# 32 bytes of padding ahead of a shared SBUF region in a two-block transformer kernel

## The chip, the cores and the metric

One core of a Trainium2 chip. The metric is the device time of one execution in microseconds; the kernel before takes 2682.19 us (median of 3 runs, 2679.93 to 2685.24).

## The reference, cut to what matters

The reference is a three-layer stack on 512 latent tokens (x) and 256 context tokens (ctx), model width 1024, everything in fp32. The first block does adaptive layer norm, windowed attention with a context, a gated delta rule in both directions, a gated merge and a squared-ReLU MLP. The second block is two layers of differential attention, a pooling mixer and the same MLP:

```
def sq_relu_mlp(h, w1, w2):
    return jnp.square(jax.nn.relu(h @ w1)) @ w2          # 1024 -> 4096 -> 1024

x = x.astype(jnp.float32) + gt1 * merge(y_attn, o_dl, dz, ga, gd)     # first block
x = x + gt2 * mlp(x, sh2, sc2)
...
for l in range(2):                                                    # second block
    u, q, k, v = split_heads(h @ w_in[l])
    ...
    x = x + ga * (mix @ w_out[l])
    x = x + gm * sq_relu_mlp(modulate(rms_norm_2(x, g_mlp[l]), sm, cm), w_mlp1[l], w_mlp2[l])
    if not last:                                                      # the same for ctx
```

So most of the arithmetic is dense products of 1024-wide activations with weights, 512 columns wide for x and 256 wide for ctx.

## The kernel before

**How a dense product is made.** Activations lie feature-major: a tensor [128, 2, 8, n] holds 8 tiles of 128 features by n tokens, twice, as a high part and a low part in fp32r (index 0 and 1 of the second axis). Weights come in blocks of 128x4096 into one of three slots of `raw` (`sync_loads`, line 301, on SP's queue). ScalarE copies a piece of 128x1024 to the high part in `ws` (line 318), VectorE subtracts to get the low part (line 326), and TensorE multiplies (`product`, line 328 on, matmul at line 337): for each of 8 k-tiles three matmuls, high by high, high by low, low by high, each with a weight load of its own.

```
for a, b in ((lh, rh), (lh, rl), (ll, rh)):
    m = e.matmul(o, a, b, start=n == 0, stop=n == 3 * kt - 1)
```

The first operand `a` is the stationary one (128x128), the second `b` is the moving one (512 or 256 columns). The profile writes a matmul as `ps<-moving,stationary`. A piece is thus 24 matmuls of 512 columns for x, and 24 of 256 for ctx where both streams run. `pe_tiles` (lines 367 to 369) and the parts of products that run beside attention (lines 949 to 951 and 2463 to 2465) make the same three matmuls from other lines. At line 2190 the roles are turned: the weights `ws` move (512 columns) and slices of the activations `hh` or `hc` are stationary.

**Where things lie.** `build` allocates fixed tensors one after another, and behind them one region of 73728 bytes a partition, which every stage lays out anew (`region`, line 138): `ar` and `ar2` (loose fp32 scratch: q, k, v, softmax rows, delta rule), `hc1`/`hc2` (the normed ctx, shown as `hc`), `gg`/`g2` (the hidden layer of the MLPs and the merge's input, shown as `gg` and `g`), `gc2` (hidden layer of ctx, shown as `gc`), `yy` (the merged output) and `ctx2`. The program's own addresses, bytes from the start of a partition:

| tensor | address | modulo 64 |
|---|---|---|
| raw, ws, hh, xT, cst | 16512, 65664, 90240, 123008, 139392 | 0 |
| rs, sq, mi | 149056, 151104, 155200 | 0 |
| the region: ar, ar2, hc1, gg, g2 | 155232 | 32 |
| yy and gc2; hc2; ctx2 | 188000; 204384; 220768 | 32 |

`mi` is 32 bytes long, so what follows it begins 32 bytes past a multiple of 64. Every tensor of the region and every slice of 16 floats' step in it is therefore 32 bytes off; the fixed ones are not, but for `par2`, a small table of parameters.

**The order of the work.** Each engine's program is a Python function that runs through the stages in turn; the order is written out by hand, and semaphore waits are the only link between engines. The two engines that prepare `ws` work up to three pieces ahead (`WSN = 3`). Stages by the trace: inputs and q, k, v of the first block (0 to 140 us), attention (to 310), delta rule (to 635), merge and output (to 815), the first MLP (to 1181), then for each layer of the second block products, attention, output product, MLP: 1181 to 2050 with both streams, and 2050 to 2676 with x alone.

Of the kernel before, what the change touches and what calls it, by code (L numbers as in the profile page):

```python
# [15 lines left out]
P = 128  # L16
# [85 lines left out]
def build(nc, I, out):  # L102
    ctx = ExitStack()
    with ctx:
# [15 lines left out]
        def sb(name, shape, dt=F32, stack=ctx):  # L120
            return stack.enter_context(nc.sbuf_tensor(name, shape, dt))
# [11 lines left out]
        rs = sb("rs", [P, T])  # L133
        sq = sb("sq", [P, 2, T])
        mi = sb("mi", [P, 8])
        REST = 18432

        def region(names):
            st = ExitStack()
            got = [sb(n, s, dt, st) for n, s, dt in names]  # L140
            st.close()
            return got

        ar, = region([("ar", [P, REST], F32)])
        hc1, = region([("hc1", [P, 2, KT, TC], F32R)])
        gg, yy = region([("gg", [P, 2, KT, T], F32R), ("yy", [P, 2, KT, T], F32R)])
        ar2, hc2, ctx2 = region([("ar2", [P, REST - 6144], F32), ("hc2", [P, 2, KT, TC], F32R),
                                 ("ctx2", [P, KT, TC], F32)])
# [421 lines left out]

        YA = REST - 2048
        cx = ar[:, YA:YA + 2048].rearrange("p (k n) -> p k n", k=KT)
# [2429 lines left out]
```

## Time and profile before

| | |
|---|---|
| median of 3 runs | 2682.19 us (2679.93 to 2685.24) |
| span of the profiled execution, first to last instruction | 2676.4 us |
| median less span | 5.8 us |
| mean granted TensorE clock | 0.978 |
| busy: PE, VectorE, ScalarE, GpSimd | 94%, 58%, 35%, 4% |
| chain that ended last: PE, VectorE, ScalarE, DMA | 85%, 9%, 2%, 1% |

The span is the profiler's, from the first to the last instruction; the runs' times take in what lies around it. A matmul's duration in the trace is not its share of the engine: matmuls are pipelined, each one's record lasts until its last column is out, and the next has begun long before. What a matmul costs in a saturated stretch is the distance from one start to the next, and in the view in order of time it is found as (start of the next row less start of this one) divided by the count of this row.

### The profile page before, as it was taken

The page shows a single profiled execution, that of the slowest core. Times are in us where ns is not written, and L with a number is a line of the kernel's source. Part 1 is how long each engine was busy: PE and PEld are TensorE (multiplying, and loading weights), DVE is VectorE, ACT ScalarE, POOL GpSimd, SP SyncE. Part 2 cuts the span into 40 slices and gives each one's busy share as a digit, 9 for nine tenths or more (in the row PEclk, how much of TensorE's full clock was granted, in tenths as well). Part 3 has the DMA queues.
Part 4 walks back from the last instruction along what each step waited for, and adds up shares of the span by engine and source line. Part 5 has one row for each costly group of instructions (what it writes and reads, how often), then busy time and mean ns, then how long its engine had stood idle before and what let it go on. Part 6 is the DMA issues. An engine that isn't in the chain of part 4 may idle for free.

```text
span 2676.4 us, 45804 instructions
## 1 busy us (share of the span) xinstructions
PE 2521.2 (94%) x19622; PEld 2039.4 (76%) x19622; DVE 1557.1 (58%) x2412; ACT 931.9 (35%) x1599; POOL 115.6 (4%) x222
## 2 busy tenths in 40 slices
PE   6999988779999999999998999999999998999997
PEld 3777667667887788877777888888887776788886
DVE  3355577767656788854675556545445466534444
ACT  3344443223235223342553432222233254422322
POOL 0000001120100010000000000000000000000000
PEclk8999899989999999999999999999999999999999
DMA  6000000004653555411002123333321102222210
GB/s 277 32 32 1 33 3 4 5 5 172 221 214 118 181 189 190 172 44 59 5 32 79 64 95 126 126 126 126 126 95 44 63 32 86 93 97 103 95 63 32
DMA packets 32202, 244.88 MB, mean 91 GB/s; under 512 B 3616, under 2 KB 3776, under 8 KB 20992
## 3 DMA queue, kind: packets, MB, share of 16 engines
q1 hardware_dynamic: 11808, 164.83, 15.4%
q0 software_dynamic: 20192, 77.11, 9.1%
q8 instruction: 157, 2.57, 0.4%
q14 instruction: 45, 0.37, 0.0%
HBM read 239.83 MB, written 2.10 MB: 90 GB/s over the span
## 4 chain that ended last, share of the span: by engine, by line
PE 85%; DVE 9%; issue 3%; ACT 2%; DMA 1%; POOL 0%; DVEq 0%; SPq 0%; ACTq 0%
PE ps L337 57%; PE ps L2190 2%; PE ps L2419 2%; PE ps L949 1%; PE ps L2447 1%; PE ps L1370 1%; PE ps L2463 1%; PE ps L905 1%; PE ps L367 1%; PE ps L2465 1%; PE ps L2464 1%; PE ps L368 1%; PE ps L369 1%; PE ps L950 1%; PE ps L951 1%
## 5 line engine op out<-in xcount | busy, mean ns | idle before, releaser
L337 PE MATMUL ps<-hh,ws 128*128 128x512 f32 x3216 | 752.9, 393 | 10.9 <-DVE hh L524 7.1
L337 PEld LDWEIGHTS ps<-hh,ws 128*128 128x128 f32 x3216 | 601.3, 188 | 144.9 <-issue 15.6
L318 ACT ACTIVATE ws<-raw 128x1024 fp32r<-128x1024 f32 x295 | 308.6, 1049 | 430.0 <-PE ps L337 396.6
L326 DVE TENSOR_TENSOR ws<-raw,ws 128x1024 fp32r<-128x1024 f32 x295 | 359.8, 1221 | 151.5 <-ACT ws L318 151.4
L337 PE MATMUL ps<-g,ws 128*128 128x512 f32 x1536 | 364.4, 396 | 0.0
L337 PEld LDWEIGHTS ps<-g,ws 128*128 128x128 f32 x1536 | 286.4, 188 | 66.6
L337 PE MATMUL ps<-gg,ws 128*128 128x512 f32 x960 | 227.6, 398 | 2.1 <-ACT ws L318 2.1
L1807 DVE SCALAR_TENSOR_TENSOR xT<-ps,mods,xT 128x512 f32<-128x512 f32 x120 | 90.0, 750 | 227.8 <-PE ps L337 220.5
L337 PEld LDWEIGHTS ps<-gg,ws 128*128 128x128 f32 x960 | 181.3, 189 | 46.4 <-ACT ws L318 2.5
L1970 DVE TENSOR_TENSOR sq<-sq 128x512 f32<-128x512 f32 (+1 forms) x128 | 80.0, 625 | 142.4 <-ACT sq L1947 142.4
L1947 ACT ACTIVATE sq<-ps 128x512 f32<-128x512 f32 (+1 forms) x128 | 69.4, 542 | 258.7 <-PE ps L337 244.6
L337 PEld LDWEIGHTS ps<-hc,ws 128*128 128x128 f32 (+1 forms) x1032 | 129.2, 188 | 6.8 <-ACT hc L506 1.5
L337 PE MATMUL ps<-hc,ws 128*128 128x256 f32 (+1 forms) x1032 | 132.2, 284 | 1.4 <-ACT hc L506 1.1
L1880 DVE CUSTOM_DVE_ANT_0 ar<-ar,par 128x1024 f32<-128x1024 f32 x96 | 122.8, 1279 | 3.5
L337 PEld LDWEIGHTS ps<-gc,ws 128*128 128x128 f32 x768 | 95.4, 188 | 2.8
L337 PE MATMUL ps<-gc,ws 128*128 128x256 f32 x768 | 96.0, 281 | 0.0
L468 ACT ACTIVATE sq<-xT 128x512 f32<-128x512 f32 x48 | 30.3, 632 | 184.1 <-DVE xT L1807 184.1
L2638 DVE TENSOR_REDUCE mvec<-ps 128x1 f32<-128x768 f32 (+1 forms) x80 | 64.3, 846 | 51.7 <-PE ps L2419 51.3
L2564 ACT ACTIVATE raw<-ps,mvec 128x768 f32<-128x768 f32 (+1 forms) x80 | 64.5, 811 | 70.5 <-DVE mvec L2638 70.5
L1880 DVE CUSTOM_DVE_ANT_0 raw<-raw,par 128x1024 f32<-128x1024 f32 x64 | 81.9, 1279 | 2.8 <-DVE mods L1880 0.5
L1621 ACT ACTIVATE raw<-ps 128x512 f32<-128x512 f32 x60 | 35.5, 592 | 106.4 <-PE ps L1387 81.4
L1974 DVE TENSOR_TENSOR g<-sq,g 128x512 fp32r<-128x512 f32 x64 | 44.3, 693 | 44.8 <-ACT g L1950 44.8
(378 smaller groups left out, 3571.1 us busy)
## 6 DMA issues: line engine op xcount, KB each, us to landing
raw<-in_w_m SPq DMA_DIRECT2D x32, 2048.0 KB, 7.8
raw<-in_w_ada POOLq DMA_DIRECT2D x80, 512.0 KB, 3.9
raw<-in_w_mlp SPq DMA_DIRECT2D x16, 2048.0 KB, 8.0
ar<-in_w_ada POOLq DMA_DIRECT2D x48, 512.0 KB, 3.9
raw<-in_w_in SPq DMA_DIRECT2D x8, 2048.0 KB, 7.4
raw<-in_w_mg SPq DMA_DIRECT2D x8, 1536.0 KB, 7.3
raw<-in_w_out SPq DMA_DIRECT2D x6, 2048.0 KB, 8.1
raw<-in_w SPq DMA_DIRECT2D x5, 2048.0 KB, 7.5
```

What stands on the lines that cost most here:

```text
L318: e.activation(w_of(n)[0], pieces[n][2], ACT.Copy).then_inc(*hi(n))
L326: e.tensor_tensor(l, pieces[n][2], h.bitcast(F32), ALU.subtract).then_inc(*lo(n))
L337: m = e.matmul(o, a, b, start=n == 0, stop=n == 3 * kt - 1)
L1807: e.scalar_tensor_tensor(x[:, mt, 0:w], ps[name][:, 0:w], gain, x[:, mt, 0:w], ALU.mult, ALU.add).then_inc(*dve(name))
L1880: e.tensor_tensor_reduce(junk, w[t % n], cb[:, j * 1024:j * 1024 + 1024], 1.0, Q2("bada", l)[:, t:t + 1], ALU.mult, ALU.add, mods[:, 1 + l ...
L1947: e.activation(r, ps[tag, "u", q, m, j][:, 0:w], ACT.Relu).then_inc(*act((tag, "u", q, m, j)))
L1970: e.tensor_tensor(r, r, r, ALU.mult).then_inc(*dve((tag, "r2", i)))
L1974: e.tensor_tensor(hid[:, 1, m, :], r, hid[:, 0, m, :].bitcast(F32), ALU.subtract).then_inc(*dve(((tag, "hid", q, j), m)))
L2190: mm = e.matmul(ps[l, "v", i], a, b[:, kk, :], start=k == 0 and a is xh and b is h, stop=k == 7 and a is xl)
L2419: m = e.matmul(ps.two((l, "s2", i, p))[:, a:b], q, kall[halves(p), t4, a:b], start=True, stop=True)
L2564: e.activation((e_buf[i % 2], e_second)[p][:, 0:n], ps.two((l, "s2", i, p))[:, 0:n], ACT.Exp, bias=(nm0, nm1)[p], accum_out=(su0, su1)[p]) ...
L2638: e.reduce_max(nm[p], ps.two((l, "s2", i, p))[:, 0:cols_of(i)], AXX, negate=True).then_inc(*dve((l, "m2", i, p)))
```

## The change

One tensor is allocated that nothing writes or reads. It is 8 floats, 32 bytes a partition, between `mi` and the region.

```
--- before.py
+++ after.py
@@ -133,6 +133,7 @@
         rs = sb("rs", [P, T])
         sq = sb("sq", [P, 2, T])
         mi = sb("mi", [P, 8])
+        sb("line", [P, 8])
         REST = 18432
 
         def region(names):
```

By the program's own addresses `line` gets 155232, the region now begins at 155264, and all that lies in it is 32 bytes further on: yy and gc2 at 188032, hc2 at 204416, ctx2 at 220800, all multiples of 64. Everything ahead of it stays where it was. No instruction is added, removed or moved, on any engine or queue; line numbers from 136 on are one higher.

## Rows read from the trace of the kernel before

**Rows 1.** The page: busy time by engine, and the chain that ended last by engine.
```profile
PE 2521.2 (94%) x19622; PEld 2039.4 (76%) x19622; DVE 1557.1 (58%) x2412; ACT 931.9 (35%) x1599; POOL 115.6 (4%) x222
...
PE 85%; DVE 9%; issue 3%; ACT 2%; DMA 1%; POOL 0%; DVEq 0%; SPq 0%; ACTq 0%
```

**Rows 2.** The chain in order of time, its longest pieces (start, us, what).
```profile
914.33 172.99 PE ps L337 x744
...
1519.65 516.87 PE ps L337 x2964
...
2316.43 254.15 PE ps L337 x1104
```

**Rows 3.** Busy time by stretch: us and instructions, granted clock, DMA share, GB/s.
```profile
1800.00:2000.00 200.00, 200.00 (x1150) 175.45 (x1148) 98.10 (x148) 53.31 (x82) 10.55 (x20) 1.00 0.35 119
```

**Rows 4.** PE in order of time, last MLP: start us, us, op, shape, count.
```profile
2348.91 44.96 PE L337 MATMUL ps<-g,ws 128*128 128x512 f32 x192
2393.71 43.71 PE L337 MATMUL ps<-hh,ws 128*128 128x512 f32 x192
2437.25 44.96 PE L337 MATMUL ps<-g,ws 128*128 128x512 f32 x192
```

**Rows 5.** PE in order of time, end of the merge and the output product.
```profile
746.81 11.07 PE L337 MATMUL ps<-hh,ws 128*128 128x512 f32 x48
757.71 5.76 PE L337 MATMUL ps<-gg,ws 128*128 128x512 f32 x24
763.31 44.96 PE L337 MATMUL ps<-yy,ws 128*128 128x512 f32 x192
```

**Rows 6.** PE in order of time, value product of the second block, line 2190.
```profile
1216.61 2.95 PE L2190 MATMUL ps<-ws,hc 128*128 128x512 f32 x12
1219.40 5.61 PE L2190 MATMUL ps<-ws,hh 128*128 128x512 f32 x24
1224.85 2.95 PE L2190 MATMUL ps<-ws,hc 128*128 128x512 f32 x12
```

**Rows 7.** PE in order of time, MLP with both streams.
```profile
1561.07 5.65 PE L337 MATMUL ps<-hh,ws 128*128 128x512 f32 x24
1566.56 3.00 PE L337 MATMUL ps<-hc,ws 128*128 128x256 f32 x24
1569.40 5.76 PE L337 MATMUL ps<-g,ws 128*128 128x512 f32 x24
```

**Rows 8.** Groups by form, TensorE: count, busy us, mean ns, idle before.
```profile
L337 PE MATMUL ps<-g,ws 128*128 128x512 f32 x1536 | 364.4, 396 | 0.0
...
L337 PE MATMUL ps<-gg,ws 128*128 128x512 f32 x960 | 227.6, 398 | 2.1 <-ACT ws L318 2.1
...
L337 PE MATMUL ps<-hc,ws 128*128 128x256 f32 x1008 | 129.2, 284 | 1.4 <-ACT hc L506 1.1 <-DVE hc L524 0.2
...
L337 PE MATMUL ps<-gc,ws 128*128 128x256 f32 x768 | 96.0, 281 | 0.0
...
L2190 PE MATMUL ps<-ws,hc 128*128 128x512 f32 x96 | 24.4, 403 | 0.0
...
L2464 PE MATMUL ps<-hc,ws 128*128 128x256 f32 x72 | 20.2, 281 | 0.0
```

**Rows 9.** Groups by form, plain fp32 products and transposes of the attention.
```profile
L2447 PE MATMUL ps<-raw,ar 128*128 128x128 f32 x416 | 53.5, 276 | 1.3 <-ACT raw L2573 1.3
...
L2432 PE MATMUL ps<-cst,raw 128*128 128x128 f32 x208 | 30.2, 273 | 4.4 <-ACT ar L2582 2.5 <-DVE mvec L2648 1.2 <-DVE raw L2654 0.7
```

**Rows 10.** Groups by form, VectorE: one operation on either kind of tensor.
```profile
L1880 DVE CUSTOM_DVE_ANT_0 ar<-ar,par 128x1024 f32<-128x1024 f32 x96 | 122.8, 1279 | 3.5
...
L1880 DVE CUSTOM_DVE_ANT_0 raw<-raw,par 128x1024 f32<-128x1024 f32 x64 | 81.9, 1279 | 2.8 <-DVE mods L1880 0.5
...
L1970 DVE TENSOR_TENSOR sq<-sq 128x512 f32<-128x512 f32 x96 | 66.4, 692 | 125.9 <-ACT sq L1947 125.9
...
L1974 DVE TENSOR_TENSOR g<-sq,g 128x512 fp32r<-128x512 f32 x64 | 44.3, 693 | 44.8 <-ACT g L1950 44.8
```

**Rows 11.** The page, DMA issues: KB each, us from issue to landing.
```profile
raw<-in_w_ada POOLq DMA_DIRECT2D x80, 512.0 KB, 3.9
...
ar<-in_w_ada POOLq DMA_DIRECT2D x48, 512.0 KB, 3.9
```

More of the change, by code:

```diff
@@ L135, in build @@
         mi = sb("mi", [P, 8])
+        sb("line", [P, 8])
         REST = 18432
```

## Prediction, made before the changed kernel ran

> **What bounds the kernel now.** I read the page first, then the chain, then the work of TensorE in order of time. The page has TensorE busy 94% of the span, and the chain that ended last is 85% TensorE, 9% VectorE, 1% DMA [rows 1]. The chain in order of time says where: its longest pieces are the dense products of line 337, and in them the chain doesn't leave TensorE for 173, 517 and 254 us [rows 2]. In one stretch of 200 us inside the longest, TensorE is busy all 200 at a granted clock of 1.00, VectorE 98, ScalarE 53, the DMA engines 35% [rows 3]. In these stages nothing but the rate of the matmuls counts, and each nanosecond of a matmul comes through to the end.
>
> The change adds no instruction and moves none. It shifts the region by 32 bytes. So the one question is whether an engine or a DMA reads or writes a tensor faster at a multiple of 64 bytes than 32 bytes off it. The trace of before can answer it, since it has both kinds of tensor under the same operations.
>
> **TensorE, 512 columns.** In the last MLP stretches of 192 matmuls with `g` moving (32 off) alternate with 192 with `hh` moving (a multiple of 64). Same line, same shape, same weights buffer, no idle time. `g`: (2393.71 - 2348.91) / 192 = 233.3 ns each; `hh`: (2437.25 - 2393.71) / 192 = 226.8 ns [rows 4]. The difference is 6.5 ns, 2.8%. Is it the address or the phase of the MLP? In the merge the two alternate piece by piece: `hh` (757.71 - 746.81) / 48 = 227.1 ns, `gg` (763.31 - 757.71) / 24 = 233.3 ns; and `yy`, another tensor of the region with other work beside it, has 44.96 us for 192 matmuls, to the hundredth what `g` has [rows 5, 4]. The best control is line 2190, where the activations are the stationary operand and the moving one is `ws` both times: with slices of `hc` (32 off) (1219.40 - 1216.61) / 12 = 232.5 ns, with slices of `hh` (1224.85 - 1219.40) / 24 = 227.1 ns [rows 6]. So it is enough that either operand is 32 off. I take the 6.5 ns of the longest stretches.
>
> How many: 1536 with `g`, 960 with `gg`, 192 with `yy`, 96 with `hc` stationary [rows 8, 5], 2784 in all, with no idle time before them but 2.1 us. Saved: 2784 x 6.5 ns = 18.1 us. The operands after it have the same place against 64 bytes as `hh` and `ws` have now.
>
> A rule that speaks against a part of it: the Trainium skill, "SBUF — State Buffer", section "Who interferes with whom", gives TensorE two read ports, one for the moving operand and one for weight loads, independent of each other. By that the 96 matmuls with only the stationary operand off would have nothing to gain, and this term would be 17.5 us. The rows of line 2190 speak against it.
>
> **TensorE, 256 columns.** 1008 with `hc` and 768 with `gc` at line 337, and nine rows like that of line 2464 (three of 72, three of 64, three of 48, 552 matmuls) [rows 8]: 2328. All of them move a tensor that is 32 off, at (1569.40 - 1566.56) / 24 = 118.3 ns [rows 7]; no row shows one at a multiple of 64, so this price is bounded. Upper end: the same 6.5 ns for each, a fixed cost of a start, 15.1 us. Other end: 512 columns at 2.4 GHz are 213.3 ns, so an aligned matmul of 512 pays 13.5 ns over its columns, one that is off 20.0, and the narrow one pays 118.3 - 106.7 = 11.6. If the 13.5 were a fixed price of an aligned matmul, the narrow one would go to 120.2, 1.9 ns slower, a loss of 4.4 us. Between them I take the price in proportion to the columns, half of 6.5 or 3.3 ns: the narrow matmul's 11.6 is near half of the wide one's 20.0, not near the whole. 2328 x 3.3 = 7.7 us. The 360 of them at lines 949 to 951 and 2463 to 2465 stand among attention steps that wait for softmax, so I leave their 1.2 us out: 6.5 us.
>
> **TensorE, plain fp32.** The products of the second attention with a stationary operand in `ar` take 276 ns in the record, transposes of the same size with both operands in fixed tensors 273 [rows 9]. At most 416 x 3 ns = 1.2 us; half of it is on the path at best, 0.6 us. The small matmuls of the delta rule (64 columns) have no like pair, and their stage waits for VectorE step by step; nothing is put down for them.
>
> **A side effect.** After a run of `hc` the next run of `hh` takes (1566.56 - 1561.07) / 24 = 228.8 ns, not 226.8 [rows 7, 4]. It may go too: with 32 pieces of this kind and 24 matmuls each, 2 ns is 1.5 us. It stays out of the sum and in the range.
>
> **VectorE, ScalarE, DMA.** The modulation's dot product takes 1279 ns on `ar` (32 off) and 1279 on `raw` (a multiple of 64) [rows 10], and a transfer of 512 KB lands 3.9 us after its issue in either [rows 11]. Nothing to gain, nothing to lose.
>
> **What is late next.** Per piece of 24 wide matmuls TensorE's time falls from 5.60 to 5.44 us. In the stretch of rows 3 VectorE has half of its time free, so pieces of weights stay ahead and no new wait comes up.
>
> **The sum.** 18.1 + 6.5 + 0.6 = 25.2 us off the profiled execution's span of 2676.4, which gives 2651.2. The median of the runs lies 5.8 us above that span: 2657.0 us, 0.9% faster.
>
> **The rivals.**
>
> *The narrow matmuls gain nothing, or lose.* The terms are then 18.1 + 0.6, less 4.4 at the worst: between 2663.5 and 2667.9 us. For it speaks that their 11.6 ns over the columns are already under the 13.5 of an aligned wide one. Against it, that 20.0 for 512 columns and 11.6 for 256 look like a cost that grows with the columns.
>
> *Nothing changes.* The 6.5 ns would come from where the region lies (all of it is above 155000 bytes) or from something that I haven't thought of that its tensors share. Then the time is 2682.2 us. All tensors of the region are both 32 off and high up, so no row of TensorE separates the two fully; but `g`, `yy` and `hc` lie up to 49 KB apart and cost the same to within 1 ns, which doesn't look like a matter of distance. That the allocation does nothing is ruled out by the program's own addresses.
>
> Beside it a rule: the Trainium skill, "SBUF — State Buffer", section "Specifications (TRN2)", gives SBUF cachelines of 16 bytes. 32 bytes are two whole lines, so by that rule no operand crosses more lines before than after and this rival is right. The rows of TensorE speak against 16 bytes being the only unit that counts.
>
> *Slower: the clock gives it back.* The saturated stretches get 2.8% denser in columns, and if TensorE's granted clock fell there, all matmuls in them would pay. The place is the three stretches of rows 2, 944 us; 0.01 of clock costs 9.4 us, so it decides from a fall of 0.027 on, and a fall of 0.04 would give 2657.0 + 37.6 = 2695 us. Against it: the `hh` stretches already run at this density, and the stretch of rows 3, with TensorE busy all the time, has a granted clock of 1.00.
>
> **How the numbers follow.** Forecast as summed, 0.72. Narrow ones without gain, 0.15. No change, 0.10. Clock, 0.03. The range: the full 6.5 ns for the narrow ones adds 8.6 us, all of the fp32 term 0.6, the side effect 1.5, which is 2646; a little more for the runs' own spread of 3 us gives 2644. Upward the second case reaches 2668, and with that spread 2670. No change and slower are outside, 0.13. Of a measurement of this kernel about 0.2%, 5.4 us, can be told from no change: faster by more than that has the first two cases, 0.87; within it, no change, 0.10; slower, 0.03.
>
> **What would show it.** In the profile after, the `g` stretches of the last MLP should take 43.5 us from start to start for 192 matmuls, as `hh`, not 44.8; line 2190 should show no difference between `hc` and `hh`; a narrow run of 24 should take 2.76 us from start to start (2.84 would be the second case, 2.68 the upper end). VectorE's 1279 ns and the 3.9 us should stand. I am wrong in the mechanism if `g` still takes 233 ns, and wrong in the path if the matmuls get faster and idle time before them takes up what they save, which rows on line 337 with a new wait for `ws` would show.

## The result, and the profile after

The changed kernel takes 2666.3 us (median of 4 runs, 2665.1 to 2670.61), the kernel before 2681.78 us beside it (4 runs, 2679.93 to 2685.24). The ratio is 0.9954, with a 95% interval of 0.9941 to 0.9968: 12.3 us less, between 8.6 and 15.8. The interval leaves out 1, so it is faster, and the time is inside the range, but the gain is about half of the 25 us that were forecast. The profiled execution took 2665.17 us with a span of 2663.4, 13.0 us under the span of before.

The page after: TensorE's busy time is 16.4 us less, and the chain that ended last is on TensorE for 84% of the span, where it was 85%.

```profile
PE 2504.8 (94%) x19622; PEld 2040.8 (77%) x19622; DVE 1556.6 (58%) x2412; ACT 931.4 (35%) x1599; POOL 115.6 (4%) x222
...
PE 84%; DVE 9%; issue 3%; ACT 2%; DMA 1%; POOL 0%; DVEq 0%; ACTq 0%; POOLq 0%
```

The chain in order of time, the three pieces that answer to [rows 2]. They are 2.6, 2.5 and 3.9 us shorter; the middle one, 517 us with narrow matmuls in it, gained least for its length.

```profile
910.43 170.37 PE ps L338 x744
...
1512.01 514.34 PE ps L338 x2964
...
2308.58 250.25 PE ps L338 x1104
```

Busy time in the stretch of [rows 3]. TensorE is as full as it was at a granted clock of 1.00, with VectorE and ScalarE where they were: in this stretch the clock gave nothing back.

```profile
1800.00:2000.00 200.00, 200.00 (x1153) 177.04 (x1152) 97.22 (x145) 52.33 (x80) 10.03 (x19) 1.00 0.33 116
```

TensorE in order of time in the last MLP (start us, us, engine, line, operation, shape, count), which answers to [rows 4]:

```profile
2341.06 43.68 PE L338 MATMUL ps<-g,ws 128*128 128x512 f32 x192
2384.58 43.68 PE L338 MATMUL ps<-hh,ws 128*128 128x512 f32 x192
2428.10 43.68 PE L338 MATMUL ps<-g,ws 128*128 128x512 f32 x192
```

`g` now has (2384.58 - 2341.06) / 192 = 226.7 ns from start to start, as `hh` has, where it had 233.3.

The value product, now line 2191, for [rows 6]: with `hc` stationary (1211.68 - 1208.96) / 12 = 226.7 ns, where it had 232.5.

```profile
1208.96 2.88 PE L2191 MATMUL ps<-ws,hc 128*128 128x512 f32 x12
1211.68 5.60 PE L2191 MATMUL ps<-ws,hh 128*128 128x512 f32 x24
```

The MLP with both streams, for [rows 7]:

```profile
1553.52 5.63 PE L338 MATMUL ps<-hh,ws 128*128 128x512 f32 x24
1558.99 3.04 PE L338 MATMUL ps<-hc,ws 128*128 128x256 f32 x24
1561.86 5.63 PE L338 MATMUL ps<-g,ws 128*128 128x512 f32 x24
```

Here is the surprise: a narrow run of 24 takes 1561.86 - 1558.99 = 2.87 us, 119.6 ns a matmul, where it had 118.3. It got slower.

The groups by form, TensorE (count, busy us, mean ns, idle before), for [rows 8]:

```profile
L338 PE MATMUL ps<-hh,ws 128*128 128x512 f32 x3192 | 745.8, 392 | 11.0 <-DVE hh L525 7.3 <-DVE xT L1808 3.1 <-issue 0.5
...
L338 PE MATMUL ps<-g,ws 128*128 128x512 f32 x1536 | 355.3, 390 | 0.0
...
L338 PE MATMUL ps<-gg,ws 128*128 128x512 f32 x960 | 221.5, 391 | 2.1 <-ACT ws L319 2.1
...
L338 PE MATMUL ps<-hc,ws 128*128 128x256 f32 x1008 | 129.6, 284 | 1.9 <-ACT hc L507 1.1 <-DVE hc L525 0.7
...
L338 PE MATMUL ps<-gc,ws 128*128 128x256 f32 x768 | 97.0, 283 | 0.0
```

From before to after: `g` 364.4 to 355.3, `gg` 227.6 to 221.5, `yy` 45.0 to 43.7, line 2190 with `hc` 24.4 to 23.9 us busy, together 17.0 us less; `hh` 746.8 to 745.8; `hc` 129.2 to 129.6 and `gc` 96.0 to 97.0, 1.4 us more. That is 16.6 us less. The other 552 narrow ones, which stand among steps that wait, show no loss: their groups are busy 166.0 us before and 165.4 after. In the MLP with both streams `g` behind a narrow run takes 227.9 ns after, not 226.7; that is why the wide ones gained 17.0 us and not 18.1.

The span fell by 13.0 us, 3.6 less than the 16.6. In another profiled execution of the same changed kernel (below) the span was 2659.4 us, 4.0 less, and all of these 4.0 lie ahead of 911 us; from there on the two agree to 0.1 us. So a part of the 3.6 can't be told from chance, but one place repeats: from the end of the longest piece of the chain to the value product of the next layer it was 34.2 us before (2036.5 to 2070.7) and is 35.7 in both executions after. A dip of the granted clock lies in it each time, at another place: in the two stretches of 6 us that begin 7.5 us behind the piece it is 0.53 and 0.90 before, 0.75 and 0.78 after. That this is what the 1.6 us are is not shown.

### The profile page after: what moved, and what is told of

It is laid out like the page before. It is cut to its first block, busy times and chain, and to the rows that moved or that the text cites. A ratio compares the mean times of both kernels' runs of the same rounds, so it can differ in the third digit from the quotient of the medians.

```text
span 2663.4 us, 45804 instructions
## 1 busy us (share of the span) xinstructions
PE 2504.8 (94%) x19622; PEld 2040.8 (77%) x19622; DVE 1556.6 (58%) x2412; ACT 931.4 (35%) x1599; POOL 115.6 (4%) x222
## 3 DMA queue, kind: packets, MB, share of 16 engines
q1 hardware_dynamic: 11808, 164.83, 15.5%
## 4 chain that ended last, share of the span: by engine, by line
PE 84%; DVE 9%; issue 3%; ACT 2%; DMA 1%; POOL 0%; DVEq 0%; ACTq 0%; POOLq 0%
PE ps L338 56%; PE ps L2191 2%; PE ps L2420 2%; PE ps L950 1%; PE ps L2448 1%; PE ps L1371 1%; PE ps L2464 1%; PE ps L368 1%; PE ps L906 1%; PE ps L370 1%; PE ps L369 1%; PE ps L2466 1%; PE ps L2465 1%; PE ps L952 1%; PE ps L951 1%
## 5 line engine op out<-in xcount | busy, mean ns | idle before, releaser
L338 PE MATMUL ps<-g,ws 128*128 128x512 f32 x1536 | 355.3, 390 | 0.0
L338 PE MATMUL ps<-gg,ws 128*128 128x512 f32 x960 | 221.5, 391 | 2.1 <-ACT ws L319 2.1
L1881 DVE CUSTOM_DVE_ANT_0 ar<-ar,par 128x1024 f32<-128x1024 f32 x96 | 122.8, 1280 | 3.5
L1881 DVE CUSTOM_DVE_ANT_0 raw<-raw,par 128x1024 f32<-128x1024 f32 x64 | 81.9, 1279 | 2.8 <-DVE mods L1881 0.5
L1371 PE MATMUL ps<-ar,raw 64*64 64x64 f32 x1920 | 44.4, 230 | 29.1 <-DVE ar L1569 22.1
```

What stands on the lines that cost most here:

```text
L1371: m = e.matmul(ps.two(name)[halves(j), 512 * p + 64 * b:512 * p + 64 * b + 64], A[halves(p), 2 * b + j, :], Xt[halves(p), 2 * b + j, :], s ...
L1881: e.tensor_tensor_reduce(junk, w[t % n], cb[:, j * 1024:j * 1024 + 1024], 1.0, Q2("bada", l)[:, t:t + 1], ALU.mult, ALU.add, mods[:, 1 + l ...
```

## The experiments

All kernels keep every instruction in its place and move only addresses, unless said otherwise. "Distance" is the moving operand's address less the stationary one's, modulo 256 bytes; `ws` lies at 128 past a multiple of 256, so it is 224 for the region of before (155232, 96 past a multiple of 256), and 0 for the changed kernel's (155264, 128 past one). In the value product, where the region's tensor is the stationary one, it was 32 before and is 0 after. I came to look at it that way only after the first two kernels.

**Only the wide tensors moved (mixed), and only the narrow ones (reverse).** Mixed:

```
-        sb("line", [P, 8])
...
+        hc1, = region([("hc1", [P, 2, KT, TC], F32R)])
+        sb("line", [P, 8])
         ar, = region([("ar", [P, REST], F32)])
-        hc1, = region([("hc1", [P, 2, KT, TC], F32R)])
...
+        ar2, _, hc2, _, ctx2 = region([("ar2", [P, REST - 6144], F32), ("off1", [P, 8], F32),
+                                       ("hc2", [P, 2, KT, TC], F32R), ("off2", [P, 8], F32),
+                                       ("ctx2", [P, KT, TC], F32)])
+        g2, _, gc2 = region([("g2", [P, 2, KT, T], F32R), ("off3", [P, 8], F32), ("gc2", [P, 2, KT, TC], F32R)])
```

> The changed kernel, but with the ctx tensors of the products (hc1, hc2, gc2) put 32 bytes off again; gg, g2, yy, ar, ar2, ctx2 stay at multiples of 64. Theory A, each matmul's cost depends on where its own operands lie: 512-column matmuls stay at 227 ns, 256-column ones at line 337 go from 120.0 back to 118.4 ns, the 96 with hc stationary from 227 back to 233. 2328 x 1.6 = 3.7 us less, 0.5 us more: the span is some 3 us under the changed kernel's 2663.4, the ratio to before 0.994. Theory B, the narrow matmuls got slower because what runs between them got faster (a rhythm of the engine, not their own address): they stay at 120.0 and the time is the changed kernel's, 2666.

Measured: 2661.44 us, ratio 0.9936 (0.9924 to 0.9947). TensorE in order of time:

```profile
1557.15 5.63 PE L339 MATMUL ps<-hh,ws 128*128 128x512 f32 x24
1562.62 2.96 PE L339 MATMUL ps<-hc,ws 128*128 128x256 f32 x24
1565.42 5.63 PE L339 MATMUL ps<-g,ws 128*128 128x512 f32 x24
```

The wide ones stay at 227.9 ns or less, and the narrow ones take (1565.42 - 1562.62) / 24 = 116.7 ns. Theory B as I put it then, that they would stay at 120.0, falls. But 116.7 is also less than the 118.4 of theory A. The tensors are 32 off a multiple of 64 as before, yet hc2 and gc2 are now at distance 32, not 224.

Reverse has one more 32 bytes, between hc1 and `ar`:

```
+        sb("line", [P, 8])
+        hc1, = region([("hc1", [P, 2, KT, TC], F32R)])
+        sb("line2", [P, 8])
         ar, = region([("ar", [P, REST], F32)])
```

and the rest as in mixed, so that hc1, hc2, gc2 are at multiples of 64 and the others 32 off.

> The opposite: only the ctx tensors of the products (hc1, hc2, gc2) lie at multiples of 64; gg, g2, yy, ar, ar2, ctx2 are 32 bytes off as before. Theory A: 512-column matmuls with g, gg and yy at 233.3 ns, 256-column ones at 120.0 ns, those with hc stationary at 227: before plus 3.7 us less 0.5 us, some 3 us slower than before (2685, ratio 1.001). Theory B: narrow ones at 118.4 ns and the time of before, less 0.5 us.

Measured: 2673.43 us, ratio 0.9984 (0.9973 to 0.9994). That is faster than before, not slower, and the trace shows a value that neither theory has:

```profile
1574.22 5.75 PE L340 MATMUL ps<-g,ws 128*128 128x512 f32 x24
1579.81 2.88 PE L340 MATMUL ps<-gc,ws 128*128 128x256 f32 x24
1582.53 5.75 PE L340 MATMUL ps<-g,ws 128*128 128x512 f32 x24
```

`g` takes 5.59 us for 24, 232.9 ns, as expected. `gc`, at a multiple of 64, takes (1582.53 - 1579.81) / 24 = 113.3 ns, not 120. And the matmuls of the value product with `hc` stationary, at a multiple of 64, take 233.3 ns from start to start ((1224.71 - 1221.91) / 12), not 227:

```profile
1221.91 2.96 PE L2193 MATMUL ps<-ws,hc 128*128 128x512 f32 x12
1224.71 5.63 PE L2193 MATMUL ps<-ws,hh 128*128 128x512 f32 x24
```

So the place against 64 bytes isn't the rule. gc2 lies at 188096 there, 192 past a multiple of 256: its distance to `ws` is 64.

**The changed kernel once more (again),** beside these two:

> The changed kernel as it is, once more beside the two others: 0.994 to 0.997 of before by both theories. It says how far 3 us can be told here.

Measured: 2668.04 us, ratio 0.9957 (0.9944 to 0.9971). The ratio repeats to 0.0003. The intervals of mixed and of this one overlap by a little (0.9924 to 0.9947, and 0.9944 to 0.9971). The profiled execution had a span of 2659.4.

**Matmuls alone (micro).** The reference's computation is left out.

> Only matmuls: the computation of the reference is left out, x is copied to the output. Products of 12 matmuls with a weight load each, as in line 337 (fp32r, high and low part), 96 a cell, for 512, 384, 256 and 128 columns, the moving operand 0, 16, 32, 48 and 64 bytes past a multiple of 128, the stationary one 0 and 32. Nothing else runs. Theory A (address alone): 512 columns with both at 0 take 227 ns, with either 32 off 233; 256 columns 120.0 and 118.4. If 64 bytes are the unit, 16 and 48 cost what 32 costs and 64 what 0 costs; if 16 bytes are, all cost the same. Theory C (the 6.5 ns need other engines' traffic on SBUF): every offset takes 227 ns. By a fixed price of an aligned matmul, 384 columns take 160 + 13.4 = 173 ns.

```profile
139.90 22.55 PE L58 MATMUL ps<-me,wa 128*128 128x512 f32 x96
162.29 22.56 PE L58 MATMUL ps<-ma,wb 128*128 128x512 f32 x96
184.69 22.34 PE L58 MATMUL ps<-mb,wb 128*128 128x512 f32 x96
```

The first row is the moving tensor `me` with `wa` ((162.29 - 139.90) / 96 = 233.2 ns), the next `ma` with `wb` (233.3). No wide cell came under 231 ns. The reason is a slip of mine: the weights tensor `wa` itself began 64 past a multiple of 128 and `ma` too, each at another distance than I meant, and by their addresses none of the cells was at distance 0. It does rule out theory C: with nothing else running, the cells cost 231 to 235 ns, so the dear price needs no other engine's traffic. 384 columns took 173 to 177 ns there, 160 being their time at 2.4 GHz: 173 is what a fixed price of 13.4 ns gives, but no cell at distance 0 tests it. The 256-column cells took 113.3 to 119.9 ns, and those of 128 columns 111.1 to 111.7 in all nine that can be read, whatever their addresses. So at 256 columns a matmul with its weight load costs only 2 to 9 ns more than with half the columns, and a price "over the columns" is a poor measure of it.

**A region at a multiple of 64, 64 bytes further on (shift64).**

```
-        sb("line", [P, 8])
+        sb("line", [P, 24])
```

> The changed kernel with 96 bytes of padding in place of 32: the region begins at 155328, a multiple of 64 but 64 past a multiple of 128 (in the changed kernel it is a multiple of 128, as ws and hh are). If 64 bytes are the unit, all is as in the changed kernel: g, gg and yy at 227 ns, narrow ones at 120.0, ratio 0.996. If 128 bytes are, g, gg and yy stay at 231 to 235 ns as with the region 32 off, as the micro kernel's cells with a stationary operand at 64 past 128 do (233 ns), and with the narrow ones at 113 to 118 ns the ratio is 0.997 to 1.000.

Measured: 2665.17 us, ratio 0.9941 (0.9929 to 0.9953). Last MLP, then both streams:

```profile
2340.36 44.13 PE L338 MATMUL ps<-g,ws 128*128 128x512 f32 x192
2384.32 43.73 PE L338 MATMUL ps<-hh,ws 128*128 128x512 f32 x192
```

```profile
1564.00 2.99 PE L338 MATMUL ps<-hc,ws 128*128 128x256 f32 x24
1566.83 5.67 PE L338 MATMUL ps<-g,ws 128*128 128x512 f32 x24
1572.33 2.88 PE L338 MATMUL ps<-gc,ws 128*128 128x256 f32 x24
1575.05 5.66 PE L338 MATMUL ps<-g,ws 128*128 128x512 f32 x24
```

`g` takes 43.96 us for 192, 229.0 ns: neither 226.7 nor 233. `gc` takes (1575.05 - 1572.33) / 24 = 113.3 ns, `hc`, at the same distance of 64, (1566.83 - 1564.00) / 24 = 117.9. Both readings of my expectation are wrong on the wide ones, and the total comes out level with the changed kernel, since what the wide ones lose the narrow ones give.

**The narrow tensors apart, first try (narrow64).** Mixed with 16 floats in place of 8 in the three gaps, 24 in `line`, and 16 behind hc1:

```
+        sb("line", [P, 24])
+        hc1, = region([("hc1", [P, 2, KT, TC], F32R)])
+        sb("line2", [P, 16])
```

> gg, g2, yy, ar, ar2, ctx2 at multiples of 128 as in the changed kernel; hc1, hc2, gc2 at 64 past a multiple of 128. In the reverse kernel gc at that place took 113.3 ns beside g at 233 ns, hc 118 to 120. Theory A (own place alone): wide ones at 227 ns, gc at 113.3, hc at 118: 768 x 6.7 + 1560 x 2 = 8 us under the changed kernel, ratio 0.993. Theory B (the engine carries a rhythm over from what ran before, so that the wide ones beside them count too): narrow ones anywhere between 113 and 120 beside the faster wide ones, at best 2328 x 6.7 = 16 us under the changed kernel (0.990), at worst its time. hc stationary at 233 ns costs 0.6 us in both.

Measured: 2675.04 us, ratio 0.9983 (0.9973 to 0.9992). `g` is slow again, at a multiple of 256:

```profile
2345.06 44.95 PE L340 MATMUL ps<-g,ws 128*128 128x512 f32 x192
2389.85 43.70 PE L340 MATMUL ps<-hh,ws 128*128 128x512 f32 x192
```

44.79 us for 192, 233.3 ns. Here gg and g2 begin at 155392, which is 0 past a multiple of 256, with `ws` at 128. Aligning the moving tensor buys nothing by itself: this address is better aligned than the changed kernel's, and costs what the address of before did. The edit also missed its aim: with the wide tensors at distance 128, hc2 and gc2, 64 bytes further on, are at 192, not 64. In the value product, where `hc` is the stationary operand, the distance is then 64, and these matmuls take (1218.97 - 1216.22) / 12 = 229.2 ns, the same half-fast value as `g` at distance 64 in shift64.

**A grid of distances (grid).** The reference's computation is left out.

> Only matmuls, the reference's computation is left out. Products of 24 as line 337 makes them, hi/lo and k strides as there, 96 a cell. Tensors begin at multiples of 256; the stationary operand is moved by 0, 32, 64, 128 bytes, the moving one by 0, 16, 32, 48, 64, 96, 128, 160, 192, 224 (one line of the kernel for each), for 512 and 256 columns; then runs of 24 wide (moved by 0 or 32) alternating with runs of 24 narrow (by 0, 32, 64, 96, 128, 192), stationary by 0. If 128 bytes are the unit, 512 columns take 227 ns at (0 or 128, 0 or 128) alone and 231 to 235 elsewhere; if 64 are, also at 64 and 192. Narrow ones: 120 ns where both are at a multiple of 128, 113 to 119 elsewhere. Theory A: in the alternating part a narrow run costs the same whether the wide one is moved by 0 or 32; theory B: it does not.

Some rows (a line for each place of the moving tensor: L55 is 0, L56 16, L57 32, L59 64, L60 96, L61 128; `wa` at 0, `wb` at 32, `wd` at 128):

```profile
46.56 21.92 PE L55 MATMUL ps<-mw,wa 128*128 128x512 f32 x96
68.32 22.40 PE L56 MATMUL ps<-mw,wa 128*128 128x512 f32 x96
...
135.35 22.15 PE L59 MATMUL ps<-mw,wa 128*128 128x512 f32 x96
157.34 22.57 PE L60 MATMUL ps<-mw,wa 128*128 128x512 f32 x96
...
291.80 21.93 PE L56 MATMUL ps<-mw,wb 128*128 128x512 f32 x96
313.57 21.96 PE L57 MATMUL ps<-mw,wb 128*128 128x512 f32 x96
...
848.49 21.95 PE L61 MATMUL ps<-mw,wd 128*128 128x512 f32 x96
870.27 22.57 PE L62 MATMUL ps<-mw,wd 128*128 128x512 f32 x96
```

From start to start, divided by 96, in ns, one row for each place of the stationary operand:

```
512 columns, moving at     0     16     32     48     64     96    128    160    192    224
stationary at   0      226.7  231.7  233.3  233.2  229.1  233.4  233.3  234.2  233.2  233.2
stationary at  32      233.2  226.8  227.1  231.6  233.4  228.9  233.4  233.3  234.2  233.2
stationary at  64      233.3  234.7  233.3  226.7  227.1  233.4  229.0  233.4  233.3  234.2
stationary at 128      233.3  233.3  234.2  231.1  233.3  233.2  226.9  233.4  229.0  233.5
256 columns
stationary at   0      119.8  118.9  116.7  118.2  117.8  120.0  118.6  117.3  113.5  118.3
stationary at  32      118.3  117.2  119.8  118.7  116.7  113.3  120.0  118.6  117.3  113.8
stationary at  64      117.8  119.2  118.2  117.2  119.9  117.8  117.8  119.9  118.6  117.4
stationary at 128      118.8  118.6  118.7  119.1  113.6  118.2  120.0  117.8  117.8  119.9
```

For 512 columns the fast cells follow the distance: 0 (226.7 to 227.1), also 16 below it (226.7, 226.8), and half fast at distance 64 (228.9 to 229.1); the rest is 231 to 235, whether it is a multiple of 64, of 128, or neither. A period of 512 is ruled out: by the program's own addresses the distance at 0 is a multiple of 512 for `wa` (37376) and `wc`, and 256 past one for `wb` and `wd`, with `mw` at 71168, and all four are fast. A longer period can't be told, since within a product the stationary slices lie 512 bytes apart and the moving ones 2048. At 256 columns distance 0 is among the worst places (119.8 to 120.0 in all four rows, and distance 96 has 119.9 to 120.0 too), and the best value, 113.3 to 113.8, comes up at distances 64 and 192, though not each time (117.8 too). What ran before counts as well at some distances, as the alternating part shows (at distances 0, 32 and 96 a narrow run costs the same behind either wide one, to 0.4 ns). A narrow run at distance 64 behind a wide one at 0, and then behind one at 32:

```profile
1456.55 5.63 PE L55 MATMUL ps<-mw,wa 128*128 128x512 f32 x24
1462.02 2.99 PE L59 MATMUL ps<-mn,wa 128*128 128x256 f32 x24
1464.85 5.64 PE L55 MATMUL ps<-mw,wa 128*128 128x512 f32 x24
```

```profile
1657.31 5.76 PE L57 MATMUL ps<-mw,wa 128*128 128x512 f32 x24
1662.91 2.88 PE L59 MATMUL ps<-mn,wa 128*128 128x256 f32 x24
1665.62 5.75 PE L57 MATMUL ps<-mw,wa 128*128 128x512 f32 x24
```

(1464.85 - 1462.02) / 24 = 117.9 ns, and (1665.62 - 1662.91) / 24 = 112.9 ns for the very same addresses. Theory A is wrong for the narrow ones taken alone: what ran before changes the price of the same addresses. The run directly before isn't all of it either: at distance 192, behind the same wide run at 32, the first of four narrow runs took 117.9 ns and the next two 113.8. What is carried over, no run here shows.

**All operands 32 off, together (together).** The test of the distance in the whole kernel:

```
+        sb("push", [P, 56])
         ws = sb("ws", [P, WSN, 2, 1024], F32R)
         hh = sb("hh", [P, 2, KT, T], F32R)
```

and `line` as in the changed kernel. `ws`, `hh` and the region all begin 96 past a multiple of 256.

> Padding of 224 bytes ahead of ws and of 32 ahead of the region, so that ws, hh and all of the region lie at 96 past a multiple of 256: every operand of line 337 is 32 bytes off a multiple of 64, but all by the same. If only the distance between the moving and the stationary operand counts, modulo 256 bytes, this is as fast as the changed kernel: hh, g, gg and yy at 227 ns, gc at 120, ratio 0.996. If the place against 64 bytes counts, hh gets as slow as g was (233 ns, some 4300 matmuls more, 28 us) and the ratio is 1.01.

Measured: 2666.56 us, ratio 0.9961 (0.9947 to 0.9976), the changed kernel's within the interval.

```profile
2342.45 43.68 PE L339 MATMUL ps<-g,ws 128*128 128x512 f32 x192
2385.97 43.68 PE L339 MATMUL ps<-hh,ws 128*128 128x512 f32 x192
2429.49 43.68 PE L339 MATMUL ps<-g,ws 128*128 128x512 f32 x192
```

43.52 us for 192 of either, 226.7 ns, with no operand at a multiple of 64. The alignment theory would have lost 28 us against before; it is settled against it.

**The narrow tensors apart, as meant (narrow64b).** Against narrow64:

```
-        sb("line2", [P, 16])
+        sb("line2", [P, 48])
```

and 8 floats in place of 16 behind hc2, which moves ctx2 alone, so that gg, g2, yy are at distance 0 and hc1, hc2, gc2 at 64.

> What the kernel narrow64 was meant to be: gg, g2, yy at distance 0 from ws modulo 256 (in narrow64 they were at 128, and slow), hc1, hc2, gc2 at distance 64. Wide ones at 227 ns. Theory A (own distance alone): gc at 113.3 as in shift64, hc 118: 8 us under the changed kernel, ratio 0.993. Theory B (what runs before counts too; in the grid a narrow run at distance 64 took 112.9 ns behind a wide one moved by 32, 117.9 behind one at 0): gc and hc at 118, 4 us under the changed kernel, 0.994 to 0.995, level with or behind the mixed kernel (0.9936).

Measured: 2663.93 us, ratio 0.9949 (0.9933 to 0.9964).

```profile
1561.61 2.99 PE L340 MATMUL ps<-hc,ws 128*128 128x256 f32 x24
1564.44 5.64 PE L340 MATMUL ps<-g,ws 128*128 128x512 f32 x24
1569.92 2.99 PE L340 MATMUL ps<-gc,ws 128*128 128x256 f32 x24
1572.75 5.64 PE L340 MATMUL ps<-g,ws 128*128 128x512 f32 x24
```

`gc` behind a fast `g` takes (1572.75 - 1569.92) / 24 = 117.9 ns, as theory B and the grid have it, where it took 113.3 behind the slower `g` of shift64 and reverse. The two can't be had at once at this distance. Here the address of `g` less that of `ws` (155520 - 65664) is 256 past a multiple of 512, where in the changed kernel (155264 - 65664) it is a multiple of 512, and `g` is as fast: its 1536 matmuls are busy 355.5 us against 355.3.

**What came out lowest.** Mixed, with the wide tensors at distance 0 and hc2 and gc2 at 32, has the lowest ratio to before, 0.9936, against 0.9957 for the changed kernel in the same series, 6.6 us by the medians. It can't be told from shift64 (0.9941) and narrow64b (0.9949), whose intervals overlap with its own, and barely from the changed kernel. What its trace shows is less: `hc` 127.7 and `gc` 94.7 us busy, 4.2 less than in the changed kernel, and 0.5 more for the 96 matmuls with `hc` stationary. These 3 to 4 us are the safer figure for the placement; the stretch between the layers, told of in the result, also happens to take 34.1 us in it and not 35.7.

## Why the prediction was half right

**Right: the place and the wide matmuls.** The dense products are bound by TensorE's rate, what they saved came through in their own stretches, and no new wait stands before them (idle before `hh` 11.0 us and before `gg` 2.1, where it was 10.9 and 2.1). The term for 512 columns was 18.1 us; it measured 17.0, at 226.7 ns as forecast where x runs alone and at 227.9 behind narrow runs. Reading the price from both kinds of tensor under one line of code held. The stationary operand's 96 matmuls fell from 232.5 to 226.7 ns, so the trace bears out the rows of line 2190. It speaks against what the prediction drew from the Trainium skill, "SBUF — State Buffer", section "Who interferes with whom", that with two independent read ports these 96 had nothing to gain. Whether a read port is what the price comes from, no run shows. VectorE's dot product (1280 and 1279 ns) and the transfers (3.9 us both) stood, as forecast.

**Wrong: the narrow matmuls.** The step that failed is "Between them I take the price in proportion to the columns". I had 3.3 ns saved on each, 6.5 us; at line 337 they got 1.3 ns slower instead, which cost 1.4 us of busy time, and the others gained nothing that can be seen. The term was about 8 us off, which is most of the 12 by which the span missed the forecast. The lower end of my own bounds, 120.2 ns for a fixed price of 13.5 ns over the columns, was nearly the value measured (119.6 to 119.8). This is the case of the first rival, which I gave 0.15, and 2666.3 us lies between its 2663.5 and 2667.9. The hint was in hand: the narrow one already paid less over its columns (11.6 ns) than an aligned wide one (13.5), which no cost that only adds to a fixed aligned base allows. That the lower end came out is in part luck, since a fixed price over the columns isn't the rule: the same 256-column matmul takes 112.9 to 120.4 ns by its distance and by what ran before, and for 128 columns 13.5 ns over the 53.3 that the columns take at 2.4 GHz would give 66.8, where micro measured 111.7.

**Small terms.** The 0.6 us for plain fp32 didn't come: line 2448 still has 276 ns and line 2433 273, so a place at a multiple of 64 doesn't remove that difference. The side effect on `hh` came by half: 5.47 us for 24 behind a narrow run, 227.9 ns, from 228.8, 1.0 us in all. Outside the sum, the profiled execution of before lay low. Its span was 2676.4, and after, an execution's own time less its span is 1.8 us, which for before would give 2678.2, under all four of its timed runs. Most of the 5.8 that I carried over is this. It put nothing wrong into the forecast of the median, but it makes the difference of the two spans (13.0) smaller than that of the medians (15.5).

**Wrong for the right size: the reason.** I took 6.5 ns as the price of being 32 bytes off a multiple of 64. The sentence "it is enough that either operand is 32 off" fitted all rows of before, because in that kernel "32 off" and "at another distance than 0 modulo 256 from the other operand" are the same tensors. `together` (all 32 off, fast), `narrow64` (a multiple of 256, slow) and the grid separate them. The change worked since its 32 bytes happened to bring the region to the same place modulo 256 as `ws`: the right size of this term is luck as far as the reason goes. The 16-byte cachelines of the Trainium skill, "SBUF — State Buffer", section "Specifications (TRN2)", would, as the prediction read them, have had no change at all; the wide matmuls, 6.6 ns faster after a shift of two whole lines, speak against that being all that counts.

**The other rivals.** No change by location: out, `g` moved 32 bytes and took 6.6 ns less. The clock: out where the rival had it, granted 1.00 in the same saturated stretch, and 0.979 over the span where it was 0.978; the dip between the layers is told above.

**Left open.** Why a distance of 0 is good for 512 columns and bad for 256, what is carried over from one run of matmuls to the next, and whether the period is 256 or something longer than 512. The delta rule's and the attention's small fp32 matmuls were not tried at other distances.

## What to carry to other kernels

Where a stream of fp32r matmuls with a weight load each bounds a kernel, look at the start-to-start time by operand pair: a tensor that costs 3% more under the same line may point to its address relative to the weights', and one dummy tensor of some bytes moves it. Choose the distance between moving and stationary operand by a measurement for each width, not by aligning: what was best for 512 columns was among the worst for 256. And when a price has bounds of both signs, don't take a value between them by proportion; ask which end the known rows forbid.

## What the runs showed of the hardware that I had not expected

- A 512-column fp32r matmul with its own weight load costs 226.7 to 227.1 ns at distance 0 modulo 256 bytes and 16 below it, 229 at 64, and 231 to 235 at the others tried, at a granted clock of 1.00, in the whole kernel and with nothing else running.
- A 256-column one costs 112.9 to 120.4 ns. Distance 0 gives 120. At distance 64 the value depends on what ran before (112.9 against 117.9 ns for the same addresses). A 128-column one costs 111.1 to 111.7 ns at every distance tried.
- An address at a multiple of 256 can be slow (233.3 ns) and one 32 bytes off any multiple of 64 fast (226.7 ns).
